# Feed-forward hidden activations of a two-block transformer kernel: made as token rows, 512 columns a pass, and turned by TensorE

## What is computed

```python
def swiglu_ffn(x, w1, w2):
    a, b = jnp.split(x @ w1, 2, axis=-1)
    return (jax.nn.silu(a) * b) @ w2
```

## Time and profile before

| | before |
|---|---|
| median of 3 runs | 2006.24 us |
| lowest, highest | 2003.27, 2014.5 us |
| the profiled execution | 2006.02 us |
| its span | 2004.3 us |
| mean granted clock of TensorE | 0.984 of 2.4 GHz |
| ACT busy | 838.6 us (42%) |
| weight loads of PE busy | 1702.1 us (85%) |
| DMA, mean over the span | 171 GB/s |

### The profile page before, as it was taken

How to read it: one execution, slowest core, us unless ns; L and a number is a source line. 1 busy time by engine, 2 the same in 40 slices (tenths; PEclk the granted TensorE clock), 3 DMA queues, 4 the chain that set the end, 5 groups by cost and what they waited for, 6 DMA issues and landing times.

```text
span 2004.3 us, 31271 instructions
## 1 busy us (share of the span) xinstructions
PE 1931.7 (96%) x11674; PEld 1702.1 (85%) x11674; DVE 1349.4 (67%) x1707; ACT 838.6 (42%) x1042; POOL 116.2 (6%) x144
## 2 busy tenths in 40 slices
PE   7989999978999999999999999989999999999998
PEld 7977888867888788888989988878888988998887
DVE  5476777744777677776566777767777666677776
ACT  4444334433433343353355443334334335544333
POOL 0000300320000000000200100000000020010000
PEclk9999999978999999999999999999999999999999
DMA  7512555411655455553433545555554443355553
GB/s 289 188 64 103 206 189 190 162 54 63 260 190 191 178 220 188 188 179 134 161 127 127 205 184 188 188 213 216 191 190 161 150 156 140 127 180 191 189 191 121
DMA packets 47607, 342.40 MB, mean 171 GB/s; under 512 B 5344, under 2 KB 5376, under 8 KB 7440
## 3 DMA queue, kind: packets, MB, share of 16 engines
q1 hardware_dynamic: 43200, 313.02, 43.5%
q0 software_dynamic: 4304, 27.95, 3.7%
HBM read 339.89 MB, written 1.05 MB: 170 GB/s over the span
## 4 chain that ended last, share of the span: by engine, by line
PE 59%; issue 33%; DVE 4%; ACT 2%; POOL 1%; DMA 0%; POOLq 0%; DVEq 0%; ACTq 0%
PE bank L981 15%; PE bank L797 10%; PE bank L799 10%; PE bank L798 10%; PE bank L980 7%; PE bank L1081 3%; PE bank L856 2%; PE bank L1055 1%; PE bank L983 1%; POOL rstd L665 1%; DVE y L1725 1%; ACT p L1464 1%; POOL mix L784 1%; DVE wlo L1679 0%; ACT whi L1340 0%
## 5 line engine op out<-in xcount | busy, mean ns | idle before, releaser
L1679 DVE TENSOR_TENSOR wlo<-raw,whi 128x2048 fp32r<-128x2048 f32 x296 | 679.4, 2298 | 269.4 <-ACT whi L1340 267.9
L981 PE MATMUL bank<-ysp,whi 128*128 128x512 f32 x1920 | 666.0, 396 | 0.0
L1340 ACT ACTIVATE whi<-raw 128x2048 fp32r<-128x2048 f32 x296 | 564.6, 1909 | 241.7 <-PE bank L799 235.9
L980 PE MATMUL bank<-ysp,wlo 128*128 128x256 f32 x1680 | 468.5, 279 | 0.0
L981 PEld LDWEIGHTS bank<-ysp,whi 128*128 128x128 f32 x1920 | 347.6, 188 | 67.1
L980 PEld LDWEIGHTS bank<-ysp,wlo 128*128 128x128 f32 x1680 | 316.7, 189 | 10.7
L1422 ACT ACTIVATE sg<-sg 128x256 f32<-128x256 f32 x120 | 50.1, 418 | 468.3 <-DVE sg L1808 468.3
L797 PE MATMUL bank<-ysp,wlo 128*128 128x256 f32 x720 | 208.9, 290 | 3.7 <-DVE nv L2129 2.0
L797 PE MATMUL bank<-whi,hl 128*128 128x512 f32 x528 | 205.9, 390 | 0.0
L799 PE MATMUL bank<-whi,hh 128*128 128x512 f32 x528 | 205.4, 389 | 0.0
L798 PE MATMUL bank<-wlo,hh 128*128 128x512 f32 x528 | 205.4, 389 | 0.0
(11 more groups left out here) (302 smaller groups left out, 2443.7 us busy)
## 6 DMA issues: line engine op xcount, KB each, us to landing
raw<-stream SPq DMA_DIRECT2D x296, 1024.0 KB, 4.8
sr<-side POOLq DMA_DIRECT2D x10, 1024.0 KB, 5.9
gbc<-gains POOLq DMA_DIRECT2D x11, 512.0 KB, 3.9
cw<-small POOLq DMA_DIRECT2D x2, 2048.0 KB, 10.0
dbias<-dilb POOLq DMA_DIRECT2D x1, 2304.0 KB, 10.2
lng<-rows POOLq DMA_DIRECT2D x2, 1024.0 KB, 5.3
tab<-second POOLq DMA_DIRECT2D x1, 1724.0 KB, 16.0
x<-xin SPq DMA_DIRECT2D x2, 512.0 KB, 6.6
```

The source lines that it names most:

```text
L980: pe.matmul(o[:, 0, :], lo[:, k, cols], yh[:, k, :], start=False, stop=False, skip_group_check=True)
L981: last = pe.matmul(o, hi[:, k, cols], ysp[:, :, k, :], start=k == 0, stop=k == 7)
L1340: act.activation(whi[s], raw[s], ACT.Copy).then_inc(hi_made, 1)
L1679: dve.tensor_tensor(wlo[s], raw[s], whi[s].bitcast(F32), ALU.subtract).then_inc(lo_made, 1)
```

## The change

Pairs 1 to 10 are made like pair 0: `up(B, i)` calls `token_pair` with the pair's two tiles, and the products by chunk, with L980, L981 and L983, are gone. The weight stream is laid out for that: a pair's two tiles hold features 0 to 511 and 512 to 1023 of all its 512 columns (`halves`) where each held all features of one chunk. The number of tiles, their size and order of use stay.

PE turns each pair's rows: the transposes of the first row half stand right behind the upward pass, those of the second behind the downward product that follows. At the start, the second half's transposes of pair 0 stand behind pair 1's pass, together with the first half's of pair 1, and down(0) follows directly. At the end, those of the second half of pair 10 stand behind the first quarter of down(9). They go to the banks 6 and 7 (4 and 5 before).

ACT makes SiLU of all pairs from the banks 0 and 1, the first half upon `row_done`, the second upon the step's end. On DVE the two reductions go, and a pair is: split, product of the first row half, split, product of the second row half, halves of the first half's turned result, split, halves of the second half's turned result. For pair 1 the second half's turned result of pair 0 comes in behind the first product.

The core of the diff:

```diff
-        self.led_by_pair(name, "DD", "DD-" * (NF // 2 - 1) + "-")
+        self.led_by_pair(name, "DD", "DD-" * (NF // 2 - 1) + "-", NF // 2)
...
+        out.row0 = self.row0 + 2 * pairs
...
-                    pe.wait_ge(drain_dve, B.drained(s0 + m + 1, "D"))
+                def hidden_turn(B, chunks, i, m):
+                    pe.wait_ge(drain_dve, B.drained(s0 + max(3 * i - 1, 0) + m + 1, "D"))
+                    if i and m == 0:
+                        pe.wait_ge(h_ready, chunks + 2 * i - 1)
                     for c in range(2):
-                        last = pe.transpose(pb[4 + m][:, c * P:c * P + P], h32[m][:, c * P:c * P + P], ident)
+                        last = pe.transpose(pb[6 + m][:, c * P:c * P + P], h32[m][:, c * P:c * P + P], ident)
                     last.then_inc(ht_done, 1)
-                def up(B, step, bank):
-                    tile = t0 + step - 1
-                    tile_split(B, tile)
...
-                    for c in range(2):
-                        o = bank2(up_banks[bank][c])
-                        for k in range(8):
-                            cols = slice(c * P, c * P + P)
-                            if k:
-                                pe.matmul(o[:, 0, :], lo[:, k, cols], yh[:, k, :], start=False, stop=False, skip_group_check=True)
-                            last = pe.matmul(o, hi[:, k, cols], ysp[:, :, k, :], start=k == 0, stop=k == 7)
-                            if k == 0:
-                                pe.matmul(o[:, 0, :], lo[:, k, cols], yh[:, k, :], start=False, stop=False, skip_group_check=True)
-                    last.then_inc(step_done, 1)
...
-                def ups(B, i):
-                    up(B, 3 * i - 1, 0)
-                    up(B, 3 * i, 1)
+                def up(B, i):
+                    token_pair(B, stage, 3 * i - 1, t0 + 3 * i - 2)
                 def pair(B, chunks, i):
-                    ups(B, i)
+                    up(B, i)
+                    hidden_turn(B, chunks, i, 0)
                     down(B, chunks, i - 1, 3 * i)
+                    hidden_turn(B, chunks, i, 1)
                 token_pair(B, stage, 0, t0, True, norm_late(B, norm_stage, n))
-                hidden_turn(0)
-                up(B, 2, 0)
-                hidden_turn(1)
-                up(B, 3, 1)
+                hidden_turn(B, NF * f, 0, 0)
+                up(B, 1)
+                hidden_turn(B, NF * f, 0, 1)
+                hidden_turn(B, NF * f, 1, 0)
                 down(B, NF * f, 0, 3)
+                hidden_turn(B, NF * f, 1, 1)
                 with nc.tensor.Fori(0, FFN_ROUNDS) as r:
                     for i in (2, 3):
                         pair(B.later(r), NF * f + 4 * r, i)
                 last_i = NF // 2 - 1
-                ups(B, last_i)
+                up(B, last_i)
+                hidden_turn(B, NF * f, last_i, 0)
                 down_ready(B, NF * f, last_i - 1, FFN_TILES - 2)
                 for i, j in ((last_i - 1, 0), (last_i - 1, 1), (last_i - 1, 2), (last_i, 0), (last_i, 1), (last_i, 2), (last_i - 1, 3), (last_i, 3)):
+                    if (i, j) == (last_i - 1, 1):
+                        hidden_turn(B, NF * f, last_i, 1)
...
-                def silu(B, gates_made, j, step):
-                    ahead(B, stage, step - 1)
-                    act.wait_ge(gate_made, gates_made + j - 1)
-                    act.activation(sg[j % 2], sg[j % 2], ACT.Silu).then_inc(silu_done, 1)
-                def pair(B, gates_made, i):
-                    silu(B, gates_made, 2 * i, 3 * i - 1)
-                    silu(B, gates_made, 2 * i + 1, 3 * i)
+                def silu(B, i, m):
+                    if m == 0:
+                        act.wait_ge(row_done, B.row(stage, i))
+                    else:
+                        stepped(B, stage, max(3 * i, 1))
+                    act.activation(sg[m], pb[m][:, 0:256], ACT.Silu).then_inc(silu_done, 1)
+                def pair(B, i):
+                    ahead(B, stage, 3 * i - 2)
+                    silu(B, i, 0)
+                    ahead(B, stage, 3 * i - 1)
+                    silu(B, i, 1)
                     ahead(B, stage, 3 * i)
...
+                silu(B, 0, 0)
+                ahead(B, stage, 0)
+                silu(B, 0, 1)
+                pair(B, 1)
...
-                def hidden(B, chunks, gates_made, i, j, step, first=False):
-                    if not first:
-                        ahead(B, stage, step - 1)
-                    gate, up = (bank2(b) for b in ((6, 7), (0, 1))[j % 2])
-                    stepped(B, stage, step)
-                    dve.tensor_reduce(sg[j % 2], gate.rearrange("p a n -> p n a"), AX_X, ALU.add).then_inc(gate_made, 1)
-                    dve.tensor_reduce(h32[j % 2], up.rearrange("p a n -> p n a"), AX_X, ALU.add).then_inc(drain_dve, 1)
-                    dve.wait_ge(silu_done, chunks + j + 1)
-                    dve.wait_ge(drain_dve, B.drained(B.plan.step[stage] + step + 1, "D"))
-                    dve.tensor_tensor(h32[j % 2], sg[j % 2], h32[j % 2], ALU.mult).then_inc(h_made, 1)
...
-                    dve.tensor_copy(hh[i % 2][:, j % 2, :], h32[j % 2]).then_inc(hh_made, 1)
-                    dve.wait_ge(hh_made, chunks + j + 1)
-                    dve.tensor_tensor(hl[i % 2][:, j % 2, :], h32[j % 2], hh[i % 2][:, j % 2, :].bitcast(F32), ALU.subtract).then_inc(h_ready, 1)
-                def pair(B, chunks, gates_made, i):
-                    hidden(B, chunks, gates_made, i, 2 * i, 3 * i - 1)
-                    hidden(B, chunks, gates_made, i, 2 * i + 1, 3 * i)
+                def row(B, chunks, i, m):
...
+                def hidden_turned(B, chunks, i, m):
+                    dve.wait_ge(ht_done, chunks + 2 * i + m + 1)
+                    src = pb[6 + m][:, 0:256].rearrange("p (c t) -> p c t", c=2)
+                    sl = (slice(None), slice(None), slice(m * P, m * P + P))
+                    dve.tensor_copy(hh[i % 2][sl], src).then_inc(hh_made, 1)
+                    dve.wait_ge(hh_made, chunks + 2 * i + m + 1)
+                    dve.tensor_tensor(hl[i % 2][sl], src, hh[i % 2][sl].bitcast(F32), ALU.subtract).then_inc(h_ready, 1)
+                def pair(B, chunks, i):
+                    ahead(B, stage, 3 * i - 2)
+                    row(B, chunks, i, 0)
+                    if i == 1:
+                        hidden_turned(B, chunks, 0, 1)
+                    ahead(B, stage, 3 * i - 1)
+                    row(B, chunks, i, 1)
+                    hidden_turned(B, chunks, i, 0)
                     ahead(B, stage, 3 * i)
...
-                def hidden_turned(m):
...
+                    hidden_turned(B, chunks, i, 1)
...
+                row(B, NF * f, 0, 0)
+                ahead(B, stage, 0)
+                row(B, NF * f, 0, 1)
+                hidden_turned(B, NF * f, 0, 0)
+                pair(B, NF * f, 1)
...
-        def up(j):
-            tiles.append(weight_tile([w1[:, P * j:P * j + P], w1[:, FF + P * j:FF + P * j + P]], D))
...
         for i in range(1, NF // 2):
-            up(2 * i)
-            up(2 * i + 1)
+            c = 2 * P * i
+            halves([w1[:, c:c + 2 * P], w1[:, FF + c:FF + c + 2 * P]], tiles)
             down(i - 1)
```

More of the change, by code:

```diff
@@ L1430, in ffn @@
                 load_table(ACT.Silu)
-                for m in range(M):
-                    if m == 0:
-                        act.wait_ge(row_done, B.row(stage))
-                    else:
-                        ahead(B, stage, 0)
-                        stepped(B, stage, 1)
-                    act.activation(sg[m], pb[m][:, 0:256], ACT.Silu).then_inc(silu_done, 1)
-                pair(B, (NF - 2) * f, 1)
+                silu(B, 0, 0)
+                ahead(B, stage, 0)
+                silu(B, 0, 1)
+                pair(B, 1)
                 with nc.scalar.Fori(0, FFN_ROUNDS) as r:
                     for i in (2, 3):
-                        pair(B.later(r), (NF - 2) * f + 4 * r, i)
+                        pair(B.later(r), i)
                 if beside:
                     beside()
-                pair(B, (NF - 2) * f, NF // 2 - 1)
+                pair(B, NF // 2 - 1)
             def attention(B, stage, groups, ag0, extra=None, after=None, between=None, turned=()):
@@ L1801, in ffn @@
             def ffn(B, stage, f, weight, n, norm_stage, then=None, dst=y, beside=None):
-                def hidden(B, chunks, gates_made, i, j, step, first=False):
-                    if not first:
-                        ahead(B, stage, step - 1)
-                    gate, up = (bank2(b) for b in ((6, 7), (0, 1))[j % 2])
-                    stepped(B, stage, step)
-                    dve.tensor_reduce(sg[j % 2], gate.rearrange("p a n -> p n a"), AX_X, ALU.add).then_inc(gate_made, 1)
-                    dve.tensor_reduce(h32[j % 2], up.rearrange("p a n -> p n a"), AX_X, ALU.add).then_inc(drain_dve, 1)
-                    dve.wait_ge(silu_done, chunks + j + 1)
```

(42 more changed lines are left out.)

5 lines of the change are left out of this document (removed).

## The result

| | before | changed |
|---|---|---|
| median of four runs on the same chips | 2008.31 us | 2031.84 us |
| lowest, highest | 2003.27, 2014.5 | 2030.5, 2034.64 |
| the profiled execution, its span | 2006.02, 2004.3 | 2030.5, 2028.7 |

The changed kernel is slower: ratio 1.0118, 95% interval 1.0085 to 1.015. The forecast was 2029 us, with a range of 2013 to 2040. Every median here leaves out slow runs; there was one, of 8164.08 us, in the experiment e4_no_turn.

The account below looks back on a forecast made before the run. PE alone was taken to bound the loop. Per feed-forward, 1.4 us (transposes less the pass's gain) plus waits of 1.0, 0.6 and 0.8 make +3.8, six +23: 2006 + 23 = 2029 us, range 2013 to 2040.

Parts of the forecast that it names:

- What bounds the loop: Feed-forward loop: PE alone sets the time, so what VectorE is spared there is worth nothing by itself.
- The pass: Upward products of a loop pair: 48 matmuls at 0.2267 take 10.88 us instead of 11.19, a gain of 0.31.
- The transposes: Four more on PE per loop pair: a group of two costs 0.225 us, a pair 0.45.
- Waits in the loop, none: Loop pairs: PE never waits for VectorE, with 3.6 us of cover for the second row half's gating product.
- Start: Before each feed-forward's first downward product: PE idles 0.90 us, with the restart 1.0; bounds 0 and 1.4.
- End: Each feed-forward's end: PE idles 0.5 us before the last transposes, 0.75 before the last pair's downward part; with restarts 0.6 and 0.8.
- Sum: Whole kernel: each feed-forward grows by 3.8 us, six by 23, from 2006 to 2029.
- Rival 1: Feed-forward waits: the order hides them and only the loop's net of 8 us stays, 2014 us; chance 0.15.
- Rival 3: Added transposes: each costs its full duration of 0.271 us, +38, so 2067 us; chance 0.05.
- rival 2: Wide upward matmuls: without the additions reading banks they run at 0.2133 us each, 39 saved, 1990; chance 0.04.
- rival 4: Transposes behind a wait: each group restarts the stream for 0.08 us, +10, so 2039 us; chance 0.09.
- rival 5: Every loop pair: PE idles 1 us because VectorE's chain comes 4.6 us later, +60, so 2089 us; chance 0.05.

Follow-up runs that it names:

- e4_no_turn: The changed kernel without the transposes of pairs 1 to 10, whose rows enter the downward product unturned; 2007.36 us, 0.9997 of the kernel before.
- e5_no_add: The kernel before, with VectorE's two reductions of each looped product replaced by copies of the bank's first half; 2009.13 us, 1.0007 of the kernel before.
- e3_double: The changed kernel with every group of two transposes issued twice, same result; 2063.21 us, 1.0265 of the kernel before.
- e11_all_warm: The changed kernel with its three waits mended and small matmuls on constants added at two places and in seven attention groups; 2013.23 us, 1.0012 of the kernel before.
- e7_pool: The changed kernel with its three waits mended and GpSimd's 32 rotary-table products held back to the first feed-forward's sixth pair; 2021.36 us, 1.006 of the kernel before.

## Why the prediction was right, point by point

- **What bounds the loop** (PE alone): right. The relief of VectorE changed nothing alone (e5_no_add), nor did it in the change.
- **The pass**: right. 10.88 us for 48 matmuls; pair without transposes 16.32 (e4_no_turn). The choice of the downward product's 0.2267 over the mixer's 0.2273 held.
- **The transposes**: mechanism right, size too small. A group costs 0.255, not 0.225. I measured up to the second matmul behind the transposes (here too 229.03 - 228.58 = 0.45, which leaves 0.22). But the next few also start 0.23 to 0.24 apart, so it takes some six matmuls until the pace is 0.2267 again: 11.13 less 10.88 is 0.25, 5.70 less 5.44 is 0.26. That is 20 x 0.03 = 0.6 us a feed-forward. Doubling them (e3_double) showed that the second pair of a group of four costs 0.23.
- **Waits in the loop, none**: right; 3.6 us of cover were counted, and PE is busy all through. The 0.7 us of cover for the second tile of the first looped pass held too: no wait stands there.
- **Start**: counted as 0.90 idle, measured 0.85 (206.20). Taking it away gave 0.4 to 1.0 a feed-forward.
- **End**: 0.5 and 0.75 idle counted, 0.39 and 0.68 measured in the first feed-forward. Taking the second away gave 0.92 where 0.8 was counted. All three gave 2.4 a feed-forward, as counted (1.0 + 0.6 + 0.8).
- **Sum**: +23 was forecast, the spans differ by 24.4 and the medians by 23.5. It is partly luck. The feed-forwards grew by 4.6 us each, not 3.8, 27.5 in all; outside them the changed kernel's profile is 3.1 shorter, 2.8 of it at the place where the clock was 1.00 and not 0.50. The term that was missing is the transposes' tail (0.6 of the 0.8); the prediction had no term for the clock.
- **Rival 1** (only the net stays, 2014) can be tested by mending the waits: that gave 2023 on the chip and 13 us over before in the feed-forwards, since the net is 2.2 a feed-forward and not 1.4. **Rival 3** fell by e3_double, **rival 2** by e4_no_turn and e5_no_add, **rivals 4 and 5** by the loop pair of 16.83 with PE busy: rival 4 would have made it 16.93, rival 5 17.8. The tail is still a small kin of rival 4, 0.03 a group where that had 0.08.

## What to carry to other kernels

Work on an engine that doesn't bound the stage was free here, and moving it to the one that does cost its whole price: four transposes a pair cost 0.51 us, against a gain of 0.31. Price a small instruction by how much later the stream behind it is, and follow the stream until its pace is back, not by its duration. And when a hand-over moves to the last moment before its reader, look at what stands ahead of it in the maker's order: a split of 2.2 us ahead of the last halves was a wait in each of six stages.

## What the runs showed of the hardware that was not expected

- The same kernel takes 2002 to 2015 us from run to run, more than the half per cent that the prediction called measurable, and the clock goes with it: the mean granted clock was 0.986 in the run of 2001.82 us and 0.978 in that of 2015.12. Much of it lies in the attention between the first and the second feed-forward: profiles with 37.5 or 41.0 us at 0.50 there take 143.2 to 144.5 us for that way, those with 54.6 us at 0.50 take 146.6 to 149.6. Filling PE's idle time with matmuls on constants (10 at two places, 5 in each of seven groups) brought that way down to 138.7 us, and the medians down by 14.6. The six runs of that kernel scatter by 2.6 us, but the twelve of e11_all_warm, with the same matmuls, by 9.9: a smaller scatter is not shown.
- A small matmul on constants in full precision (128 columns) leaves two records: 44 for 22 matmuls, and the next wide one starts 4.84 us after the first. So it costs 0.22, as much as two transposes, and how many fit in a wait has to be counted by that.
- A split of 2048 columns on VectorE, 2.29 us as a rule, took 3.00 to 5.97 us once in each of the seven profiles with token rows and GpSimd's products on tables at the old place (4.80 in the changed kernel), but 2.3 to 2.6 beside the same products in the kernel before and at their later place. In the timelines shown under e7_pool one product takes as long as the split's own work: the two engines took turns. The Trainium skill says, in "GPSIMD Engine Reference", Specifications, that the SBUF interfaces are shared with VectorE and that VectorE's instructions with two SBUF inputs contend; the split is one. The records agree with it; how long a split has to stand is not explained by any run here.
